# A 64-byte-aligned front operand, a normed operand 128 bytes further on, and two output projection tiles computed side by side

## The chip, the cores and the metric

The kernel runs on one core of a Trainium2 chip. The metric is the device time of one execution in microseconds (us); lower is better. The three runs of the kernel before gave 942.79, 944.01 and 944.62 us, so a median of 944.01 us.

## What is computed

One encoder block on 256 tokens of width 1024 in float32. Cut to what matters here:

```
n      = RMSNorm(x) * norm_mix
proj   = n @ w_in                                # 1024 x 5120: qA kA vA qB kB vB gA gB
yA, yB = differential attention, neighbourhood attention
merged = sigmoid(gA) * (yA @ w_proj_a) + sigmoid(gB) * (yB @ w_proj_b)
h      = x + merged @ w_out                      # the output projection
n2     = RMSNorm(h) * norm_ffn
q      = n2 @ peer_w_query                       # product-key router, top 16 of 16384 experts, 8 heads
y      = sum over the chosen experts of g * gelu(n2 . u_e) * v_e     # u, v: 16384 x 1024
out    = RMSNorm(h + y) * norm_final
```

The expert part is computed densely for 240 of the 256 tokens: all 128 tiles of 128 experts are multiplied with the normed tokens (the U stage), then all 128 tiles of `peer_v` with the gated results (the V stage). The other 16 tokens gather the rows of their own experts.

## The kernel before, in words

**Tiles.** All weights come as one stream of tiles, 8 chunks of 128 x 128 each, numbered `t`: tiles 0 to 39 input projection, 40 to 47 (`T_PROJ`) the two attention projections, 48 to 55 (`T_OUT`) the output projection, 56 to 71 (`T_QUERY`) the router's query, 72 to 199 (`T_U`) the U stage, then 128 tiles of the V stage. SyncE loads tile `t` into `raw` (4 slots). ScalarE makes its high part `whis` (L679), VectorE (L958) or GpSimd (L619) the remainder `wlos` = raw - high; both are rings of 4 slots. The moving operand of a stage is split in the same way, and TensorE computes three products a chunk: high x high, high weight x low operand, low weight x high operand. Each is one MATMUL with its own weight load (LDWEIGHTS), 24 of them a tile.

**Where these stand.** `split_product` (L1507) is the plain form: per chunk (whi, hi), (whi, lo), (wlo, hi), with 256 columns, or 240 in the first 42 and the last 2 tiles of the U stage. `halves_product` (L1515, L1516) is the wide form of U tiles 42 to 125: one MATMUL of 480 columns that takes high and low operand together against `whi` by the view `xpair[:, :, c, 0:NU]`, and one of 240 with `wlo`. L1819 and L1820 are the same two for the V stage, with the operand `vpair`. `token_tiles` (also L1507) turns the roles: for the V projections `xpair` is the weight and `whis`, `wlos` the moving operand.

**The operand `xpair`.** One buffer of 2 x 8 x 256 floats in each partition, high half then low half. In the front (tiles 0 to 39) it holds x scaled by the norm's gain, from tile 56 on it is written again with the normed tokens (`normed_hi` on ScalarE, `normed_low` on VectorE, through `xhi` and `xlo`), which the whole U stage reads. By the order of allocation its two halves start 192 bytes past a multiple of 256. `whis` and `wlos` start 128 past one, the operands of the projections and the query (`yhi`, `ylo`, `mhi`, `mlo`) 64 past one, `vpair` 128 past one. A chunk of 256 floats is 1024 bytes, so all chunks of an operand stand alike.

**The output projection.** Its moving operand is the merged, gated result, `mhi` and `mlo`, which VectorE and ScalarE make from each projection tile: after tile `k` VectorE runs two gating operations, the sum `mfull`, and after ScalarE's `mhi` (L786) the remainder `mlo` (L1152). The first tile, 48, is computed by `tile_arriving` (L1542, L1543, L1547): chunk by chunk, each product of `mhi` as it comes, the product of `mlo` two chunks later. Tiles 49 to 55 are plain. Tiles alternate between two PSUM banks, `pO[0]` and `pO[1]` (both halves of `pOO`), and each starts when its weights are ready (`lo_ready`) and VectorE has taken the last result of its bank (`evac_dve`, counted in `tile_wait`). After each tile VectorE adds the result to the residual in `xcol` (L1169), makes a `wlos` ahead (L958) and the low part of the next operand (L969); ScalarE makes the high part `yhi` (L691).

**PSUM.** Eight banks, in the pairs `pOO`, `pSS`, `pTT`, `pMM`. `pTT` (`pT[0]`, `pT[1]`) takes transposes in the attention and is free between the last of these and the router.

Of the kernel before, what the change touches and what calls it, by code (L numbers as in the profile page):

```python
# [27 lines left out]
F32 = mybir.dt.float32  # L28
F32R = mybir.dt.float32r
U32 = mybir.dt.uint32  # L30
ALU = mybir.AluOpType
ACT = mybir.ActivationFunctionType
AX_X = mybir.AxisListType.X

P = 128
T = 256
TB = T // P
D = 1024
C = D // P
# [5 lines left out]
PH, NK, TOPK = 8, 128, 16  # L45
# [13 lines left out]
T_OUT = T_PROJ + C  # L59
T_QUERY = T_OUT + C  # L60
# [5 lines left out]
RING = 4  # L66
# [7 lines left out]
UNITS_A, UNITS_B = 8, 8  # L74
# [33 lines left out]
NU = T - APART  # L108
# [5 lines left out]
OFFSETS_AT = 52  # L114
U_BUFS, V_BUFS = 4, 4
V_SLOT = 512
NG = NU - P
G_BLOCK = P + NK // RAW * NG
DOT_TILES = (3, 7, 16, 20, 28, 32, 41, 45)
# [61 lines left out]
def last_use(t):  # L181

    return max((x for x in range(t) if bank_of(x) == bank_of(t)), default=None)


def evac_engine(t):

    dve = lambda x: T_QB <= x < T_VB or T_GATE <= x < T_QUERY
    same = [x for x in range(t + 1) if dve(x) == dve(t)]
    return dve(t), len(same)  # L190
# [7 lines left out]
def build(nc, stream, urows, vrows, const, keys, bias, lamv, gfin, h1_dram, x_dram, a_dram, g_dram, out):  # L198
    with ExitStack() as top:
# [6 lines left out]
        def sbs(stack, name, shape, dt=F32):  # L206
            return stack.enter_context(nc.sbuf_tensor(name, shape, dt))
# [5 lines left out]
        whi = [whis[:, s] for s in range(RING)]  # L213
        wlo = [wlos[:, s] for s in range(RING)]

        with ExitStack() as front:
# [3 lines left out]
            xT = xcol[:, N_COL:N_COL + C * T].rearrange("p (c t) -> p c t", t=T)  # L220
# [8 lines left out]
            with ExitStack() as mixer:  # L229
                qkT = sbs(mixer, "qkT", [P, 16, T])  # L230
                gates = sbs(mixer, "gates", [P, 16, T])
# [36 lines left out]
                route = sbs(router, "route", [P, TB, 3, PH, TOPK])  # L268
                gsum = sbs(router, "gsum", [P, 2, TB, PH])
        G = sbs(top, "G", [P, RAW, G_BLOCK])  # L270
        held = sbs(top, "held", [P, 113, NK])
        vpair = sbs(top, "vpair", [P, RING, V_SLOT], F32R)
        small = sbs(top, "small", [P, T - P - 122, NK])
        hot_more = sbs(top, "hot_more", [P, GSUB, P], F32R)
# [27 lines left out]
        goff = small[:, 0, :].bitcast(U32)  # L302
        gval = small[:, 1, :].rearrange("p (h k) -> p h k", h=PH)
        fin = sbs(top, "fin", [P, 12])
        iota = sbs(top, "iota", [P, P])[:]
        with ExitStack() as uphase:
            xpair = sbs(uphase, "xpair", [P, 2, C, T], F32R)
            xhi, xlo = xpair[:, 0], xpair[:, 1]
            routeT = sbs(uphase, "routeT", [P, 3, P])
            ghiT = sbs(uphase, "ghiT", [P, P], F32R)  # L310
            hot1 = sbs(uphase, "hot1", [P, HOTS - 1, GSUB, P], F32R)
            ghot = sbs(uphase, "ghot", [P, HOTS - 1, GSUB, 2, P], F32R)
            ast = [sbs(uphase, f"ast{s}", [P, NU]) for s in range(AST)]
        with ExitStack() as vphase:
# [4 lines left out]
            epsc = sbs(vphase, "epsc", [P, 1])  # L319
            gfc = sbs(vphase, "gfc", [P, C])  # L320

        result = hT[:].rearrange("p (b x) t -> p b (x t)", b=TB)
        xtok = qpad[0:APART, 4:8, :].rearrange("p a t -> p (a t)")
        hots = [hot1[:, u] for u in range(HOTS - 1)] + [hot_more[:]]
# [62 lines left out]
        norm_hi = sem("norm_hi")  # L387
# [285 lines left out]
        def _(act):  # L673
# [22 lines left out]

            def normed_hi(c):
                act.wait_ge(normed, c + 1)
                act.activation(xhi[:, c, :], gates[:, c, :], ACT.Copy).then_inc(norm_hi, 1)

            def tanh_gate(j):

# [241 lines left out]
        def _(dve):  # L944
# [39 lines left out]
            def normed_low(c):  # L984
                dve.wait_ge(normed, c + 1)
                dve.wait_ge(norm_hi, c + 1)
                dve.tensor_tensor(xlo[:, c, :], gates[:, c, :], xhi[:, c, :].bitcast(F32), ALU.subtract).then_inc(norm_lo, 1)

            for half in range(2):
                dve.wait_ge(raw_landed[0] if half else head_landed, 16)  # L990
# [174 lines left out]
            for k in range(T_OUT, T_QUERY):  # L1165

                j = k - T_OUT
                dve.wait_ge(tile_done, k + 1)
                dve.scalar_tensor_tensor(xT[:, j, :], pO[k % 2][:, 0:T], 0.5, xT[:, j, :], ALU.mult, ALU.add).then_inc(evac_dve, 1)  # L1169
                dve.wait_ge(evac_dve, evac_engine(k)[1])  # L1170
                low_front(k + LEAD)
                gained_low(C, j)
                if j >= 2:
                    add_square(j - 1)
# [326 lines left out]
        def _(pe):  # L1501
            def split_product(dst, terms, opening=True, closing=True):

                last = None
                for c, (sh, sl, mh, ml) in enumerate(terms):
                    for q, (st, mv) in enumerate(((sh, mh), (sh, ml), (sl, mh))):
                        last = pe.matmul(dst, st, mv, start=(opening and c == 0 and q == 0), stop=(closing and c == len(terms) - 1 and q == 2))  # L1507
                return last
# [10 lines left out]
            def tile_wait(t):  # L1519

                pe.wait_ge(lo_ready, t + 1)
                if last_use(t) is not None:
                    by_dve, count = evac_engine(last_use(t))
                    pe.wait_ge(evac_dve if by_dve else evac_act, count)

            def tile(s, bank, mh, ml):

                return split_product(pO[bank][:, 0:T], [(whi[s][:, c, :], wlo[s][:, c, :], mh[:, c, :], ml[:, c, :]) for c in range(C)])

            def tile_arriving(t, mh, ml, high, low):  # L1530

                if last_use(t) is not None:
                    by_dve, count = evac_engine(last_use(t))
                    pe.wait_ge(evac_dve if by_dve else evac_act, count)
                s, dst = t % RING, pO[bank_of(t)][:, 0:T]
                last = None
                for c in range(C + WHOLE_LAG):
                    if c == 0:
                        pe.wait_ge(lo_ready, t + 1)
                    if c < C:  # L1540
                        pe.wait_ge(high[0], high[1] + c + 1)
                        pe.matmul(dst, whi[s][:, c, :], mh[:, c, :], start=c == 0, stop=False)  # L1542
                        pe.matmul(dst, wlo[s][:, c, :], mh[:, c, :], start=False, stop=False)  # L1543
                    e = c - WHOLE_LAG
                    if e >= 0:
                        pe.wait_ge(low[0], low[1] + e + 1)
                        last = pe.matmul(dst, whi[s][:, e, :], ml[:, e, :], start=False, stop=e == C - 1)  # L1547
                return last

            def token_tiles(s, bank, b):  # L1550
# [2 lines left out]
                return split_product(pO[bank][:, b * 2 * P:(b + 1) * 2 * P],  # L1553
                                     [(xhi[:, c, tok], xlo[:, c, tok], whis[:, s:s + 2, c, :], wlos[:, s:s + 2, c, :]) for c in range(C)])

            def square_sum(bank, k):

                pe.wait_ge(squares_added, k)
                ins = pe.matmul(bank[:, 0:T], ones[:], gates[:, 0, :], start=True, stop=k == 1)
                if k == 2:  # L1560
                    pe.wait_ge(squares, C + 1)
                    ins = pe.matmul(bank[:, 0:T], ones[:], gates[:, C - 1, :], start=False, stop=True)
                ins.then_inc(ssq_done, 1)
# [152 lines left out]
            for k in range(T_PROJ, T_OUT):  # L1716
# [3 lines left out]
                    last = split_product(pO[k % 2][:, half * T:(half + 1) * T],  # L1720
                                         [(whi[s][:, c, :], wlo[s][:, c, :], yhi[:, c, :], ylo[:, c, :]) for c in range(half * HA, (half + 1) * HA)])
                last.then_inc(tile_done, 1)
            for k in range(T_OUT, T_QUERY):
                if k == T_OUT:
                    tile_arriving(k, mhi, mlo, (m_hi, 0), (m_lo, 0)).then_inc(tile_done, 1)
                else:
                    tile_wait(k)
                    tile(k % RING, k % 2, mhi, mlo).then_inc(tile_done, 1)
            def score_keys(hp):
                if hp == 0:  # L1730
                    pe.wait_ge(keys_landed, 16)
# [48 lines left out]
            for i in range(NE_TILES):  # L1780
                if i == TURN_AT:
                    pe.wait_ge(routed, 1)
                    turn_route(1)
                k = g_step_at(i)
                s = (T_U + i) % RING
                wide_now = wide_tile(i)
                if i < WIDE_FIRST + 2:
                    tile_wait(T_U + i)
                else:
                    pe.wait_ge(lo_ready, T_U + i + 1)  # L1790
                    if i < WIDE_FIRST + 4:
                        pe.wait_ge(gbanks_free, 1)
                    else:
                        pe.wait_ge(halves_added, i - 4 - WIDE_FIRST + 1)
                dst = wide_u[(i - WIDE_FIRST) % 4] if wide_now else pO[i % 2]
                for half in range(1 if k is None else 2):
                    part = range(C) if k is None else range(half * C // 2, (half + 1) * C // 2)
                    if wide_now:
                        last = halves_product(dst, [(whi[s][:, c, :], wlo[s][:, c, :], xpair[:, :, c, 0:NU]) for c in part], 0 in part, C - 1 in part)
                    else:  # L1800
                        last = split_product(dst[:, 0:NU], [(whi[s][:, c, :], wlo[s][:, c, :], xhi[:, c, 0:NU], xlo[:, c, 0:NU]) for c in part], 0 in part, C - 1 in part)
                    if C - 1 in part:
                        last.then_inc(tile_done, 1)
                    else:

                        pe.wait_ge(gbanks_free, k + 1 if k >= 2 else 2)
                    if k is not None:
                        g_tokens(k, half)
                if i < 2:
                    score_keys(HP - 2 + i)  # L1810
# [165 lines left out]
```

## Time and profile before

| | |
|---|---|
| median of 3 runs | 944.01 us (942.79 to 944.62) |
| profiled execution, its own time | 944.44 us |
| its span, first to last instruction | 942.6 us |
| TensorE (PE) busy | 934.7 us, 99% of the span, 6660 MATMULs |
| TensorE weight loads (PEld) busy | 881.9 us, 94% |
| VectorE (DVE) busy | 783.7 us, 83% |
| ScalarE (ACT) busy | 580.4 us, 62% |
| GpSimd (POOL) busy | 343.6 us, 36% |
| mean granted clock of TensorE | 0.999 of full speed |
| chain of work that ended last | PE 94%, DVE 3%, issue 1%, ACT 1%, DMA 1% |

A MATMUL's time in the profile holds its way through the array and overlaps the next ones, so the busy time can't tell how fast products follow each other. What does is the distance from the start of one MATMUL to the start of the next, here called the **step**. It is read from start times in the timeline: over a long stretch, the difference of two starts divided by the number of MATMULs between them.

### The profile page before, as it was taken

Reading aid. Unit: us, or ns where it says so; the run is one execution under the profiler, and the core shown is the slowest. Engines: PE = TensorE matmul, PEld = TensorE weight load, DVE = VectorE, ACT = ScalarE, POOL = GpSimd, SP = SyncE. Lnnn points to the kernel's source line nnn. Section 1 sums busy time; section 2 is a strip of 40 time slices with the busy share of each in tenths; the row PEclk is TensorE's granted clock in tenths of the full one; section 3 lists DMA queues with packets and bytes.
Section 4 is the critical chain, followed back from the end, with each engine's and each line's share of the span. In section 5 each row is a group of like instructions: output and inputs, shape, how many; then the busy total and the mean of one; then the engine's idle time right before and its main releaser. Section 6 shows DMA issues by size and latency. Waiting matters only on the chain.

```text
span 942.6 us, 20282 instructions
## 1 busy us (share of the span) xinstructions
PE 934.7 (99%) x6660; PEld 881.9 (94%) x6660; DVE 783.7 (83%) x1578; ACT 580.4 (62%) x1078; POOL 343.6 (36%) x202
## 2 busy tenths in 40 slices
PE   9999999999999999999999999999999999999997
PEld 9999899999999999999999999999999999999997
DVE  7988877888799988888888987877788888888766
ACT  6555764656655547888788876655555555555545
POOL 0000000056878686888888877101100000010000
PEclk9999999999999999999999999999999999999999
DMA  8877668665688898999999998999999999999881
GB/s 300 267 235 217 202 199 237 199 218 194 186 252 234 242 255 193 254 284 285 229 257 291 236 258 248 320 346 319 319 313 319 344 330 319 319 326 313 290 267 46
DMA packets 133432, 246.55 MB, mean 262 GB/s; under 512 B 31136, under 2 KB 80160, under 8 KB 133104
## 3 DMA queue, kind: packets, MB, share of 16 engines
q1 hardware_dynamic: 110656, 227.73, 74.9%
q0 software_dynamic: 22272, 17.12, 9.5%
q8 instruction: 40, 0.66, 0.3%
q10 hardware_dynamic: 432, 0.80, 0.3%
q14 instruction: 32, 0.26, 0.1%
HBM read 219.21 MB, written 26.35 MB: 260 GB/s over the span
## 4 chain that ended last, share of the span: by engine, by line
PE 94%; DVE 3%; issue 1%; ACT 1%; DMA 1%; DVEq 0%; ACTq 0%
PE pOO L1507 29%; PE pMM L1515 8%; PE pOO L1515 8%; PE pTT L1819 6%; PE pMM L1819 6%; PE pOO L1819 6%; PE pSS L1819 6%; PE pOO L1516 4%; PE pMM L1516 4%; PE pOO L1820 3%; PE pMM L1820 3%; PE pTT L1820 3%; PE pSS L1820 3%; DVE wlos L958 1%; PE pSS L1581 1%
## 5 line engine op out<-in xcount | busy, mean ns | idle before, releaser
L679 ACT ACTIVATE whis<-raw 128x1024 fp32r<-128x1024 f32 x326 | 343.8, 1057 | 171.5 <-PE pSS L1820 145.1
L654 POOL DMA_INDIRECT g_scratch<-small x120 | 219.4, 1828 | 49.7 <-issue 35.1
L958 DVE TENSOR_TENSOR wlos<-raw,whis 128x1024 fp32r<-128x1024 f32 x172 | 208.9, 1218 | 20.0 <-ACT whis L679 19.1
L1386 DVE TENSOR_TENSOR wlos<-raw,whis 128x1024 fp32r<-128x1024 f32 x125 | 153.0, 1224 | 66.9 <-ACT whis L679 66.9
L1507 PE MATMUL pOO<-xpair,whis 128*128 128x240 f32 (+1 forms) x1184 | 205.6, 278 | 0.0
L1507 PEld LDWEIGHTS pOO<-xpair,whis 128*128 128x128 f32 x1184 | 179.0, 189 | 1.4 <-issue 1.4
L1507 PE MATMUL pOO<-xpair,wlos 128*128 128x240 f32 (+1 forms) x592 | 163.4, 276 | 0.0
L619 POOL TENSOR_TENSOR wlos<-raw,whis 128x1024 fp32r<-128x1024 f32 x30 | 72.2, 2414 | 214.4 <-ACT whis L679 214.3
L1515 PE MATMUL pMM<-xpair,whis 128*128 128x480 f32 x336 | 112.4, 379 | 0.0
L1507 PEld LDWEIGHTS pOO<-xpair,wlos 128*128 128x128 f32 x592 | 111.6, 188 | 0.0
L1515 PE MATMUL pOO<-xpair,whis 128*128 128x480 f32 x336 | 111.4, 379 | 0.0
L1516 PE MATMUL pOO<-xpair,wlos 128*128 128x240 f32 x336 | 91.2, 271 | 0.0
L1516 PE MATMUL pMM<-xpair,wlos 128*128 128x240 f32 x336 | 91.1, 271 | 0.0
L1819 PE MATMUL pTT<-vpair,whis 128*128 128x480 f32 x256 | 89.8, 375 | 0.0
L1819 PE MATMUL pMM<-vpair,whis 128*128 128x480 f32 x256 | 89.6, 374 | 0.0
L1819 PE MATMUL pOO<-vpair,whis 128*128 128x480 f32 x256 | 89.6, 374 | 0.0
L1819 PE MATMUL pSS<-vpair,whis 128*128 128x480 f32 x253 | 88.6, 374 | 0.0
L635 POOL DMA_INDIRECT held<-in_vrows,small x16 | 16.2, 1015 | 161.8 <-PE pSS L1820 161.8
L1515 PEld LDWEIGHTS pOO<-xpair,whis 128*128 128x128 f32 x336 | 63.1, 188 | 8.7
L1515 PEld LDWEIGHTS pMM<-xpair,whis 128*128 128x128 f32 x336 | 63.1, 188 | 8.3
L1820 PE MATMUL pOO<-vpair,wlos 128*128 128x240 f32 x256 | 70.4, 275 | 0.0
L1820 PE MATMUL pMM<-vpair,wlos 128*128 128x240 f32 x256 | 70.4, 275 | 0.0
(300 smaller groups left out, 2066.0 us busy)
## 6 DMA issues: line engine op xcount, KB each, us to landing
raw<-in_stream SPq DMA_DIRECT2D x199, 512.0 KB, 4.6
raw<-in_vrows SPq DMA_DIRECT2D x128, 512.0 KB, 4.7
a_scratch<-ast SPq DMA_DIRECT2D x128, 120.0 KB
held<-a_scratch SPq DMA_DIRECT2D x128, 120.0 KB, 4.8
g_scratch<-ghot SPq DMA_DIRECT2D x32, 256.0 KB, 4.3
G<-g_scratch SPq DMA_DIRECT2D x124, 64.0 KB, 4.5
biasm<-in_bias SPq DMA_DIRECT2D x8, 256.0 KB, 5.7
g_scratch<-small POOLq DMA_INDIRECT x128
```

Of the source, the lines that this page charges most:

```text
L619: pool.tensor_tensor(wlo[s], raw[s][:], whi[s].bitcast(F32), ALU.subtract).then_inc(lo_ready, 1)
L635: pool.indirect_dma_start(urow[U_BUFS + m % V_BUFS], None, picked, bass.IndirectOffsetOnAxis(uoff[:, m:m + 1], 0)).then_inc(urow_landed[U_ ...
L654: pool.indirect_dma_start(g_dram, bass.IndirectOffsetOnAxis(goff[:, n:n + 1], 0), gval[:, h, k:k + 1], None, compute_op=ALU.add).then_inc( ...
L679: act.activation(whi[s], raw[s][:], ACT.Copy).then_inc(hi_ready, 1)
L958: dve.tensor_tensor(wlo[t % RING], raw[t % RING][:], whi[t % RING].bitcast(F32), ALU.subtract).then_inc(lo_ready, 1)
L1386: dve.tensor_tensor(wlo[s], raw[s][:], whi[s].bitcast(F32), ALU.subtract).then_inc(lo_ready, 1)
L1507: last = pe.matmul(dst, st, mv, start=(opening and c == 0 and q == 0), stop=(closing and c == len(terms) - 1 and q == 2))
L1515: pe.matmul(both, sh, mv, start=opening and c == 0, stop=False)
L1516: last = pe.matmul(bank[:, 0:NU], sl, mv[:, 0, :], start=False, stop=closing and c == len(terms) - 1)
L1581: last = pe.matmul(pS[m][:, unit_columns(n)], qkT[rows, q0 + h, b * P:(b + 1) * P], qkT[rows, k0 + h, :], start=True, stop=True)
L1819: pe.matmul(wide[c], whi[s][:, c, :], gpair[s], start=opening, stop=False)
L1820: return pe.matmul(acc[c][:, 0:NU], wlo[s][:, c, :], ghi[s], start=False, stop=closing)
```

## The change

It has two parts.

**Where the operand starts.** The buffer becomes `xspan`, two rows of 8 x 256 + 32 floats, and a pad of 96 floats is put ahead of it. The front operand (`xhi`, `xlo`) begins each row, the normed operand (`xpair`) begins 32 floats (128 bytes) into each row. A row is now 8320 bytes instead of 8192. Counted past a multiple of 256 bytes:

| | front, high | front, low | normed, high | normed, low |
|---|---|---|---|---|
| before | 192 | 192 | 192 | 192 |
| now | 64 | 192 | 192 | 64 |

To make room `held` loses 4 rows that nothing reads, `iota` moves behind the operand, and `vpair`, `small` and the `hot_more` buffers move down by 2048 bytes, `hT` of the end by 2176 bytes; `hot1` and `ghot`, the operands of the 112 small products that build the gates (L1770), go from 192 to 64 past a multiple of 256. No instruction of the front or of the U and V stages is added, removed or moved.

**The output projection.** `mixed_tiles` computes tiles 48 and 49 chunk by chunk side by side, tile 48 into `pO[0]` and tile 49 into `pT[0]`. Tile 50 is plain again and goes to `pO[0]`.

```
+X_SHIFT, X_PAD = 32, 96
-        held = sbs(top, "held", [P, 113, NK])
+        held = sbs(top, "held", [P, 109, NK])
-        iota = sbs(top, "iota", [P, P])[:]
+        sbs(top, "x_pad", [P, X_PAD])
         with ExitStack() as uphase:
-            xpair = sbs(uphase, "xpair", [P, 2, C, T], F32R)
-            xhi, xlo = xpair[:, 0], xpair[:, 1]
+            xspan = sbs(uphase, "xspan", [P, 2, C * T + X_SHIFT], F32R)
+            iota = sbs(uphase, "iota", [P, P])[:]
...
+        xhi, xlo = [xspan[:, q, 0:C * T].rearrange("p (c t) -> p c t", t=T) for q in range(2)]
+        xpair = xspan[:, :, X_SHIFT:].rearrange("p q (c t) -> p q c t", t=T)
...
-                act.activation(xhi[:, c, :], gates[:, c, :], ACT.Copy).then_inc(norm_hi, 1)
+                act.activation(xpair[:, 0, c, :], gates[:, c, :], ACT.Copy).then_inc(norm_hi, 1)
...
-                dve.tensor_tensor(xlo[:, c, :], gates[:, c, :], xhi[:, c, :].bitcast(F32), ALU.subtract).then_inc(norm_lo, 1)
+                dve.tensor_tensor(xpair[:, 1, c, :], gates[:, c, :], xpair[:, 0, c, :].bitcast(F32), ALU.subtract).then_inc(norm_lo, 1)
...
-                dve.scalar_tensor_tensor(xT[:, j, :], pO[k % 2][:, 0:T], 0.5, xT[:, j, :], ALU.mult, ALU.add).then_inc(evac_dve, 1)
+                dve.scalar_tensor_tensor(xT[:, j, :], (pT[0] if j == 1 else pO[k % 2])[:, 0:T], 0.5, xT[:, j, :], ALU.mult, ALU.add).then_inc(evac_dve, 1)
...
+            def mixed_tiles():
+
+                two = (T_OUT, T_OUT + 1)
+                dst = [pO[0][:, 0:T], pT[0][:, 0:T]]
+                pe.wait_ge(evac_dve, evac_engine(last_use(T_OUT))[1])
+                pe.wait_ge(turned_taken, UNITS_A + UNITS_B)
+                for c in range(C - 1):
+                    for n, t in enumerate(two):
+                        if c == 0:
+                            pe.wait_ge(lo_ready, t + 1)
+                        pe.wait_ge(m_lo, c + 1)
+                        for q, (st, mv) in enumerate(((whi, mhi), (whi, mlo), (wlo, mhi))):
+                            pe.matmul(dst[n], st[t % RING][:, c, :], mv[:, c, :], start=c == 0 and q == 0, stop=False)
+                c = C - 1
+                pe.wait_ge(m_hi, C)
+                for n, t in enumerate(two):
+                    pe.matmul(dst[n], whi[t % RING][:, c, :], mhi[:, c, :], start=False, stop=False)
+                    pe.matmul(dst[n], wlo[t % RING][:, c, :], mhi[:, c, :], start=False, stop=False)
+                pe.wait_ge(m_lo, C)
+                for n, t in enumerate(two):
+                    pe.matmul(dst[n], whi[t % RING][:, c, :], mlo[:, c, :], start=False, stop=True).then_inc(tile_done, 1)
...
-            for k in range(T_OUT, T_QUERY):
-                if k == T_OUT:
-                    tile_arriving(k, mhi, mlo, (m_hi, 0), (m_lo, 0)).then_inc(tile_done, 1)
-                else:
-                    tile_wait(k)
-                    tile(k % RING, k % 2, mhi, mlo).then_inc(tile_done, 1)
+            mixed_tiles()
+            for k in range(T_OUT + 2, T_QUERY):
+                tile_wait(k)
+                tile(k % RING, k % 2, mhi, mlo).then_inc(tile_done, 1)
...
-                        last = split_product(dst[:, 0:NU], [(whi[s][:, c, :], wlo[s][:, c, :], xhi[:, c, 0:NU], xlo[:, c, 0:NU]) for c in part], 0 in part, C - 1 in part)
+                        last = split_product(dst[:, 0:NU], [(whi[s][:, c, :], wlo[s][:, c, :], xpair[:, 0, c, 0:NU], xpair[:, 1, c, 0:NU]) for c in part], 0 in part, C - 1 in part)
```

In the order of instructions the first place is TensorE where tile 48 ends and tile 49 begins. Before (`mhi`, `mlo` the operand, `whis`, `wlos` the weights; `m_hi`, `m_lo`, `lo_ready`, `evac_dve` the semaphores waited for):

```order
L1542 MATMUL pOO<-mhi,whis 128x256 [waits m_hi]
L1543 MATMUL pOO<-mhi,wlos 128x256
L1547 MATMUL pOO<-mlo,whis 128x256 [waits m_lo] x3
L1507 MATMUL pOO<-mhi,whis 128x256 [waits evac_dve,lo_ready]
L1507 MATMUL pOO<-mlo,whis 128x256
```

Here tile 48 waits for the last chunk of `mhi` and of `mlo` at its end, and tile 49 follows; the bank that tile 49 waits for was left by tile 47. The last two of `L1542` and its partner `L1543` are chunk 7.

The second place is TensorE at the end of the two tiles of the change and the start of tile 50 (`pOO` is tile 48, `pTT` tile 49):

```order
L1575 MATMUL pOO<-mhi,whis 128x256 [waits m_hi]
L1576 MATMUL pOO<-mhi,wlos 128x256
L1575 MATMUL pTT<-mhi,whis 128x256
L1576 MATMUL pTT<-mhi,wlos 128x256
L1579 MATMUL pOO<-mlo,whis 128x256 [waits m_lo]
L1579 MATMUL pTT<-mlo,whis 128x256
L1510 MATMUL pOO<-mhi,whis 128x256 [waits evac_dve,lo_ready]
L1510 MATMUL pOO<-mlo,whis 128x256
```

Chunk 7 now stands 42 MATMULs behind the start of tile 48 instead of 19, and between the last MATMUL of tile 48 (the first `L1579`) and tile 50, which needs that bank emptied, stands one other MATMUL. Before, a whole tile of 24 stood between two tiles of one bank.

## Rows read from the trace of the kernel before

**Rows 1.** The page: busy time, granted clock in 40 slices, chain that ended last.

```profile
PE 934.7 (99%) x6660; PEld 881.9 (94%) x6660; DVE 783.7 (83%) x1578; ACT 580.4 (62%) x1078; POOL 343.6 (36%) x202
...
PEclk9999999999999999999999999999999999999999
...
PE 94%; DVE 3%; issue 1%; ACT 1%; DMA 1%; DVEq 0%; ACTq 0%
```

**Rows 2.** Groups by form: line, engine, operation, shapes, count, busy us, mean ns, idle.

```profile
L1507 PE MATMUL pOO<-xpair,whis 128*128 128x240 f32 x704 | 118.6, 274 | 0.0
L1515 PE MATMUL pMM<-xpair,whis 128*128 128x480 f32 x336 | 112.4, 379 | 0.0
L1515 PE MATMUL pOO<-xpair,whis 128*128 128x480 f32 x336 | 111.4, 379 | 0.0
L1507 PE MATMUL pOO<-xpair,wlos 128*128 128x240 f32 x352 | 96.4, 274 | 0.0
...
L1507 PE MATMUL pOO<-xpair,whis 128*128 128x256 f32 x480 | 87.0, 282 | 0.0
```

**Rows 3.** Timeline of TensorE, input projection: start us, duration us, engine, line, operation.

```profile
12.71 0.39 PE L1507 MATMUL pOO<-xpair,whis 128*128 128x256 f32 x2
...
18.04 0.28 PE L1507 MATMUL pOO<-xpair,wlos 128*128 128x256 f32 x1
...
139.00 0.40 PE L1507 MATMUL pOO<-xpair,whis 128*128 128x256 f32 x2
```

**Rows 4.** Timeline of TensorE, tiles 40 to 56.

```profile
147.48 0.28 PE L1507 MATMUL pOO<-yhi,whis 128*128 128x256 f32 x1
...
170.09 0.28 PE L1542 MATMUL pOO<-mhi,whis 128*128 128x256 f32 x1
...
172.33 0.32 PE L1542 MATMUL pOO<-mhi,whis 128*128 128x256 f32 x1
...
173.02 0.28 PE L1507 MATMUL pOO<-mhi,whis 128*128 128x256 f32 x1
...
175.75 0.28 PE L1507 MATMUL pOO<-mhi,whis 128*128 128x256 f32 x1
...
178.36 0.28 PE L1507 MATMUL pOO<-mhi,wlos 128*128 128x256 f32 x1
...
192.07 0.28 PE L1542 MATMUL pOO<-yhi,whis 128*128 128x256 f32 x1
```

**Rows 5.** Timeline of TensorE, U stage, plain tiles: two tile starts, 29 tiles apart.

```profile
262.50 0.39 PE L1507 MATMUL pOO<-xpair,whis 128*128 128x240 f32 x2
...
340.23 0.39 PE L1507 MATMUL pOO<-xpair,whis 128*128 128x240 f32 x2
```

**Rows 6.** Timeline of TensorE, U stage, wide tiles.

```profile
520.25 0.38 PE L1515 MATMUL pOO<-xpair,whis 128*128 128x480 f32 x1
520.47 0.27 PE L1516 MATMUL pOO<-xpair,wlos 128*128 128x240 f32 x1
...
521.56 0.38 PE L1515 MATMUL pMM<-xpair,whis 128*128 128x480 f32 x1
```

**Rows 7.** Timeline of TensorE, V stage.

```profile
700.03 0.37 PE L1819 MATMUL pTT<-vpair,whis 128*128 128x480 f32 x1
700.25 0.28 PE L1820 MATMUL pTT<-vpair,wlos 128*128 128x240 f32 x1
...
701.34 0.37 PE L1819 MATMUL pOO<-vpair,whis 128*128 128x480 f32 x1
```

**Rows 8.** Timeline of VectorE around tiles 47 and 50.

```profile
172.31 0.43 DVE L1152 TENSOR_TENSOR mlo<-mfull,mhi 128x256 fp32r<-128x256 f32 x1 [0.55 <-ACT mhi L786]
...
178.67 0.42 DVE L1169 SCALAR_TENSOR_TENSOR xcol<-pOO,xcol 128x256 f32<-128x256 f32 x1 [0.63 <-PE pOO L1507]
```

**Rows 9.** Timeline of ScalarE: the last `mhi`, and `yhi` after tile 50.

```profile
171.79 0.42 ACT L786 ACTIVATE mhi<-mfull 128x256 fp32r<-128x256 f32 x1 [1.47 <-DVE mfull L1147]
...
179.13 0.51 ACT L691 ACTIVATE yhi<-xcol 128x256 fp32r<-128x256 f32 x1 [0.95 <-DVE xcol L1169]
```

## The prediction

> **What bounds the kernel now.** The page first [rows 1]: TensorE is busy 99% of the span at full granted clock in every slice, and it is 94% of the chain that ended last. VectorE, the next, is at 83% and 3% of the chain. So what counts is how fast TensorE's MATMULs follow each other, and how often they stand still. The groups by form [rows 2] say how many read the operand that is moved. In the U stage these are 704 + 352 = 1056 plain products of 240 columns (44 tiles) and 2 x 336 = 672 pairs of a 480-column and a 240-column product (84 tiles). In the input projection there are 40 tiles of 24, that is 960 products, 480 of them in the one group shown.
>
> Then the timeline, for the step from one start to the next.
>
> - Input projection, tiles 2 and 3: 12.71 to 18.04 us is 47 steps, 5.33 / 47 = 113.4 ns [rows 3]. Tiles 37 to 39: from 139.00 to 147.48 us are 72 steps, 8.48 / 72 = 117.8 ns [rows 3, 4]. Both at 192 bytes past a multiple of 256.
> - Attention projections, operand at 64: 147.48 to 170.09 us, 192 steps of 117.8 ns. Output projection from tile 49 on, also at 64: 173.02 to 192.07 us, 168 steps of 113.4 ns [rows 4].
> - U stage, plain: 262.50 to 340.23 us, 29 tiles or 696 steps, 111.7 ns [rows 5]. Wide: 520.25 to 521.56 us, four pairs, 1.31 / 4 = 0.327 us a pair; within a pair 0.22 for the wide product and 0.11 for the narrow one [rows 6].
> - V stage, operands at 128 and (narrow) 64: 700.03 to 701.34 us, four pairs, again 0.327 us a pair, again 0.22 and 0.11 [rows 7].
>
> So a 256-column product has two steps, 113.4 and 117.8 ns, and each of them occurs at 64 and at 192. It keeps one over many tiles and changes only where TensorE has stood still: tile 48 is the break between the long run at 117.8 and the long run at 113.4. And a pair takes 0.327 us at two quite different placings. That is the main fact for this change: these rows show a state that is entered at a stall, not a price of an address.
>
> **The output projection.** Before: tile 48 from 170.09 to 173.02 us is 2.93 us, and 24 steps of 117.8 ns would be 2.83, so 0.10 us was lost waiting for the last chunk of `mhi` and `mlo` (`mlo` is made from 172.31 to 172.74 us). Tile 49 ends at 175.75 us [rows 4, 8]. Now: chunk 7 is asked for 42 steps after 170.09 us, at 175.0 us, when its two parts have long been ready; that 0.10 us goes. The other added waits are for earlier events (the weights of tile 49 were made a tile earlier, the transposes are over) and cost nothing; were tile 49's weights late by some tenths, they would stall its first product by as much. The 48 products take 48 x 117.8 ns = 5.65 us, to 175.74 us.
>
> Then comes a new wait. Tile 50 goes into the bank of tile 48, whose last product started two steps before, at 175.51 us. VectorE takes a tile 0.31 us after its last start (178.36 to 178.67 us) [rows 4, 8]. From there to the engine released by it are 0.46 us (178.67 to 179.13 us) [rows 8, 9]. ScalarE's `mhi` ended at 172.21 us and the product waiting for it started at 172.33 us, 0.12 us later [rows 4, 9]; of the 0.46 us, 0.43 is the operation. So tile 50 starts at about 175.51 + 0.31 + 0.43 + 0.12 = 176.37 us, against 175.75 before: **+0.6 us**. TensorE stands for that time; nothing else hides it, as TensorE is the chain. Queued behind on VectorE are tile 49 and the `wlos` of tiles 51 and 52; it was idle 0.63 us before it took tile 50 [rows 8], so it has that much slack a tile, makes up the delay within two tiles, and I charge nothing. If it did not, tile 52 would wait for its weights by what is left, some tenths. If the 48 products went at 113.4 ns, tile 50 would start at 176.16, +0.4 us. If the tiles from 50 to 56, 168 products, fell back from 113.4 to 117.8 ns because the kick at 172.33 us is gone, that is 0.74 us more, +1.35 us in all. I take +0.6, since TensorE still gets a break there, a longer one than before.
>
> **The front operand.** 36 of its 40 tiles (all but 0 to 3) could be concerned, 864 products. Bounds: all of them go from 117.8 to 113.4 ns, 864 x 4.4 ns = -3.8 us. Or the ones that run at 113.4 now lose it: tiles 2 and 3 and the few like them, taken as five tiles, 120 x 4.4 = +0.5 us. I take 0, because the two placings, 64 and 192, stand in the rows with both steps.
>
> **The normed operand.** The high half stays at 192, only the low half goes to 64. The plain products: a step of 113.4 or 117.8 needs 256 columns, so bounds are 1056 x (117.8 - 111.7) = +6.4 us, and 1056 x (111.7 - 110) = -1.8 us, 110 being the 0.11 of the narrow product in the pairs. The pairs: the wide product could take the V stage's share without giving its narrow one's; the starts are read to 10 ns, so 672 x 5 ns = 3.4 us either way. I take 0 for both, because the sum of a pair came out alike for 192/192 and for 128/64. The V stage's 1024 pairs stay at 128 and 64, their buffer moves by a multiple of 256: 0. The 112 small products of the gates move from 192 to 64: at 4.4 ns each 0.5 us either way, taken as 0.
>
> **Sum.** 0 + 0 + 0.6 us. The profiled execution's own time of 944.44 us becomes 945.04; it stands 0.4 us over the median of the runs, so against that median it is 944.01 + 0.6 = **944.6 us**.
>
> **Rules weighed against it.** A 256-column product costs 117.8 or 113.4 ns here, and the difference is what the change could win. The Trainium skill, TensorE: Matmul & The Clock Gate, Back-to-back issue gap, gives N / 2.4 + 2.5 ns, for 256 columns 109.2 ns. The trace never reaches it in these stages; were the placing alone to blame for the rest, an estimate from that page would be 864 x 8.6 ns = 7.4 us in the front.
>
> The pairs cost the same at two placings and the 256-column products show both steps at either. The same skill, SBUF — State Buffer, Who interferes with whom, says that TensorE reads moving operand and weights through two independent ports and never waits on anyone. By that rule the placing cannot matter and the sum is the new wait alone; the trace agrees as far as 64 and 192 go, and leaves unexplained why there are two steps at all.
>
> **Rivals.**
>
> 1. *The placing does act, in the front or in the U stage* (faster). For it: something makes 4.4 ns between the two steps, the weights stand at 128, and operand and weight stream at once; high and low half at different placings is a case that no row shows. Against: the 117.8 of tiles 40 to 47 at 64. If most of the front goes to 113.4: -3.8 x 0.8 = -3.0, with the wait -2.4, so 941.6 us. If the pairs gain 5 ns instead: -3.4 + 0.6, 941.2 us. Both: 938.2 us.
> 2. *The low half at 64 slows the U stage* (slower, over 945.9 us). One mechanism: the plain product's step, now 111.7 ns, goes to the state of 117.8 because two of three products now read at different placings. Full price +6.4 + 0.6, 951.0 us; at half the tiles 947.8 us. It decides once the step exceeds 111.7 by 1.3 ns (1.3 us over 1056 products). Against: the narrow product of the V stage reads at 64 and its pair is no longer.
> 3. *The states fall otherwise*: nothing depends on the placing, but each break gets another outcome. Front -1 to +0.5 us, output projection +0.4 to +1.35 us: 943.5 to 945.9 us. This is within the forecast's side.
> 4. *The new wait isn't there*, if TensorE needed no fresh bank. The order speaks against it; the time would be 943.9 us, no measurable change either.
>
> **How the numbers follow.** 0.2% of this kernel, 1.9 us, is what a measurement can tell from no change. The forecast with rivals 3 and 4: 0.45. Rival 1: 0.35. Rival 2: 0.20. The predicted time is the forecast's, 944.6 us. Its own range is 943.5 to 945.9. The range for 8 in 10 takes in rival 1 to somewhat under its two single sizes, 940.8, which leaves out the double one (about 0.1), and rival 2 to nearly half its tiles, 947.5, which leaves out about 0.1.
>
> **What would show it.** Right: tile 50 starts 0.6 us later than 175.75 counted from tile 48's start, with TensorE waiting for VectorE's L1172 on `pOO`; the waits at the end of tile 48 are gone; the mean of the front's 256-column products with `whis` stays near the 282 ns of before [rows 2]; pairs still take 0.327 us, and 29 plain U tiles 77.7 us. Wrong: a front whose mean falls by some 4 ns with a step of 113.4 throughout; pairs under 0.322 or over 0.332 us; a plain U step other than 111.7.

## The result and the profile after

| | before | changed |
|---|---|---|
| median of 6 runs | 943.44 us (942.57 to 944.62) | 947.65 us (947.21 to 948.27) |
| profiled execution, own time | 944.44 us | 947.26 us |
| its span | 942.6 us | 945.4 us |

The ratio is 1.0045 with an interval of 1.0032 to 1.0058: the change costs 4.2 us, between 3.0 and 5.5. The forecast was 944.6 us and its range ended at 947.5.

The page after, the same lines as in [rows 1]:

```profile
PE 937.0 (99%) x6660; PEld 882.4 (93%) x6660; DVE 784.6 (83%) x1578; ACT 581.2 (61%) x1078; POOL 344.1 (36%) x202
...
PEclk9999999999999999999999999999999999999999
...
PE 94%; DVE 3%; issue 1%; ACT 1%; DMA 1%; DVEq 0%; ACTq 0%
```

Nothing there says what happened: the same engine bounds the kernel, at the same clock, over the same number of instructions. The groups by form, which answer to [rows 2], say a little more. Lines have moved by three (L1515 is now L1518, L1507 L1510), `xpair` is now called `xspan`:

```profile
L1518 PE MATMUL pOO<-xspan,whis 128*128 128x480 f32 x336 | 113.1, 382 | 0.0
...
L1510 PE MATMUL pOO<-xspan,whis 128*128 128x256 f32 x480 | 87.4, 284 | 0.0
```

The 480-column products into `pOO` last 382 ns on the mean instead of 379. A mean duration moves by less than the step does, so the step has to be read from starts. The timeline of TensorE in wide tiles after the change, where [rows 6] had four pairs in 1.31 us:

```profile
543.54 0.38 PE L1518 MATMUL pOO<-xspan,whis 128*128 128x480 f32 x1
...
544.87 0.38 PE L1518 MATMUL pOO<-xspan,whis 128*128 128x480 f32 x1
```

Four pairs take 1.33 us. The whole wide stage, from its first product to the first one of the V stage, before:

```profile
359.80 0.38 PE L1515 MATMUL pOO<-xpair,whis 128*128 128x480 f32 x1
...
597.77 0.38 PE L1819 MATMUL pTT<-vpair,whis 128*128 128x480 f32 x1
```

and after:

```profile
359.50 0.38 PE L1518 MATMUL pOO<-xspan,whis 128*128 128x480 f32 x1
...
600.55 0.38 PE L1842 MATMUL pTT<-vpair,whis 128*128 128x480 f32 x1
```

237.97 us have become 241.05, that is +3.1 us. Two such rows a stage give the whole account, and every stage time below is read in this way. Times are in us, from the first MATMUL of a stage to the first of the next. The front counts from the start of the span, "two" is the start of tile 48 to the start of tile 50, the query holds the router too, the wide stage also holds the last two plain tiles, and "V and end" goes to the start of the last MATMUL:

| run | front | attn. proj. | two | tiles 50-55 | query | U plain | U wide | V and end |
|---|---|---|---|---|---|---|---|---|
| before | 147.48 | 22.61 | 5.66 | 16.32 | 53.38 | 114.35 | 237.97 | 339.63 |
| changed | 147.47 | 22.61 | 6.31 | 16.41 | 52.18 | 114.52 | 241.05 | 339.64 |
| difference | -0.01 | 0.00 | +0.65 | +0.09 | -1.20 | +0.18 | +3.08 | +0.01 |

The differences add up to +2.8 us, as the two spans do. The medians say 4.2, so this pair of profiles flatters the change. The column to distrust is the query, where nothing was changed and 1.2 us went away.

The output projection looks as forecast. TensorE, then VectorE:

```profile
175.50 0.28 PE L1579 MATMUL pOO<-mlo,whis 128*128 128x256 f32 x1
176.39 0.36 PE L1510 MATMUL pOO<-mhi,whis 128*128 128x256 f32 x1 [0.49 <-DVE xcol L1172]
```

```profile
175.82 0.42 DVE L1172 SCALAR_TENSOR_TENSOR xcol<-pOO,xcol 128x256 f32<-128x256 f32 x1 [1.82 <-PE pOO L1579]
```

The two tiles run through, VectorE takes tile 48 as soon as it is there, and tile 50 waits for it until 176.39 us. Before it started at 175.75 us [rows 4].

Two accounts of the +3.1 us stand against each other. **Placing**: the pair of a 480- and a 240-column product costs more because the normed operand's low half stands elsewhere against the weights. **State**: TensorE is in a slower state there, handed on from the new stall, and the placing has nothing to do with it.

### The profile page after: what moved, and what is told of

Same layout as the page of the kernel before. It is cut to its first block, busy times and chain, and to the rows that moved or that the text cites. A ratio compares the mean times of both kernels' runs of the same rounds, so it can differ in the third digit from the quotient of the medians.

```text
span 945.4 us, 20283 instructions
## 1 busy us (share of the span) xinstructions
PE 937.0 (99%) x6660; PEld 882.4 (93%) x6660; DVE 784.6 (83%) x1578; ACT 581.2 (61%) x1078; POOL 344.1 (36%) x202
## 4 chain that ended last, share of the span: by engine, by line
PE 94%; DVE 3%; issue 1%; ACT 1%; DMA 1%; DVEq 0%; ACTq 0%
PE pOO L1510 29%; PE pOO L1518 8%; PE pMM L1518 8%; PE pTT L1842 6%; PE pMM L1842 6%; PE pOO L1842 6%; PE pSS L1842 6%; PE pOO L1519 4%; PE pMM L1519 4%; PE pOO L1843 3%; PE pMM L1843 3%; PE pTT L1843 3%; PE pSS L1843 3%; DVE wlos L961 1%; PE pSS L1606 1%
## 5 line engine op out<-in xcount | busy, mean ns | idle before, releaser
L1510 PE MATMUL pOO<-xspan,whis 128*128 128x240 f32 (+1 forms) x1184 | 206.2, 279 | 0.0
L1510 PEld LDWEIGHTS pOO<-xspan,whis 128*128 128x128 f32 x1184 | 179.4, 189 | 1.4 <-issue 1.4
L1510 PE MATMUL pOO<-xspan,wlos 128*128 128x240 f32 (+1 forms) x592 | 164.1, 277 | 0.0
L1518 PE MATMUL pMM<-xspan,whis 128*128 128x480 f32 x336 | 113.7, 381 | 0.0
L1518 PE MATMUL pOO<-xspan,whis 128*128 128x480 f32 x336 | 113.1, 382 | 0.0
L1510 PEld LDWEIGHTS pOO<-xspan,wlos 128*128 128x128 f32 x592 | 112.4, 190 | 0.0
L1519 PE MATMUL pOO<-xspan,wlos 128*128 128x240 f32 x336 | 92.2, 274 | 0.0
L1519 PE MATMUL pMM<-xspan,wlos 128*128 128x240 f32 x336 | 92.0, 274 | 0.0
L1518 PEld LDWEIGHTS pOO<-xspan,whis 128*128 128x128 f32 x336 | 64.1, 191 | 9.5
L1518 PEld LDWEIGHTS pMM<-xspan,whis 128*128 128x128 f32 x336 | 63.8, 190 | 8.9
L1843 PE MATMUL pTT<-vpair,wlos 128*128 128x240 f32 x256 | 70.4, 275 | 0.0
```

Source lines behind the costliest of these rows:

```text
L1518: pe.matmul(both, sh, mv, start=opening and c == 0, stop=False)
L1519: last = pe.matmul(bank[:, 0:NU], sl, mv[:, 0, :], start=False, stop=closing and c == len(terms) - 1)
L1843: return pe.matmul(acc[c][:, 0:NU], wlo[s][:, c, :], ghi[s], start=False, stop=closing)
```

## The experiments

**One part each.** The placing alone takes the output projection back to that of before:

```
-            mixed_tiles()
-            for k in range(T_OUT + 2, T_QUERY):
-                tile_wait(k)
-                tile(k % RING, k % 2, mhi, mlo).then_inc(tile_done, 1)
+            for k in range(T_OUT, T_QUERY):
+                if k == T_OUT:
+                    tile_arriving(k, mhi, mlo, (m_hi, 0), (m_lo, 0)).then_inc(tile_done, 1)
+                else:
...
```

Expected:

> The change's placing alone (front 64/192, normed 192/64 past a multiple of 256, for high/low half); the output projection as before. Theory 'placing': the wide pairs of the U stage take 0.332 to 0.333 us instead of 0.327, 672 of them make +3.2 us, the output projection takes as long as before, so about 946.6 us against 943.4. Rival 'state': the slower pair is a state that the new stall at tile 50 handed on; then pairs are back at 0.327 us here and the time is that of before within 1 us.

Measured: 947.93 us against 943.85, ratio 1.0041 (1.0029 to 1.0053), 1.3 us more than the 946.6 expected. The wide stage took 241.31 us, and every stage ahead of the U stage took what it did before, within 0.04 us:

```profile
359.96 0.38 PE L1518 MATMUL pOO<-xspan,whis 128*128 128x480 f32 x1
...
601.27 0.38 PE L1844 MATMUL pTT<-vpair,whis 128*128 128x480 f32 x1
```

The other part alone is the kernel before with `mixed_tiles` put in. Expected:

> Tiles 48 and 49 side by side alone, every buffer where it was. Theory 'placing': pairs stay at 0.327 us; tile 50 starts 0.7 us later than before, and the query tiles get back up to 1.1 us as in the changed kernel (they read the same operand at the same place), so 943.0 to 944.2 us. Rival 'state': pairs take 0.332 us and the time is near 946.6 us.

Measured: 944.52 us against 943.85, ratio 1.0011 (1.0002 to 1.0019), so about +1 us and 0.3 us above the expected range. The wide stage took 237.98 us. The wait at tile 50 is there as in the changed kernel:

```profile
175.13 0.28 PE L1576 MATMUL pTT<-mlo,whis 128*128 128x256 f32 x1
175.90 0.36 PE L1507 MATMUL pOO<-mhi,whis 128*128 128x256 f32 x1 [0.49 <-DVE xcol L1169]
```

So the wide stage's +3.1 to +3.3 us belongs to the placing and comes without the new stall; the state theory falls. The two parts' ratios, +0.41% and +0.11%, add up to the whole's +0.45% within their intervals.

**Which half, and against what.** Next the row length: with 64 floats behind each row instead of 32, high and low half stand alike, front 64/64 and normed 192/192.

```
-            xspan = sbs(uphase, "xspan", [P, 2, C * T + X_SHIFT], F32R)
+            xspan = sbs(uphase, "xspan", [P, 2, C * T + X_ROW], F32R)      # X_ROW = 64
```

> As the first, but each row is 256 bytes longer than 8 x 256 floats, so high and low half stand alike: front 64/64, normed 192/192. Theory 'placing of the low half': pairs are back at 0.327 us, the plain U tiles at 2.680 us, and the time at that of before, 943.4 us (a front at 64/64 changes it by less than 1 us). Rival 'the row length or the move of the buffer as such costs': pairs stay at 0.332 us, 946.6 us.

Measured: 943.92 us, ratio 0.9995 (0.9986 to 1.0004); the wide stage took 238.35 us:

```profile
359.12 0.37 PE L1518 MATMUL pOO<-xspan,whis 128*128 128x480 f32 x1
...
597.47 0.38 PE L1844 MATMUL pTT<-vpair,whis 128*128 128x480 f32 x1
```

The buffer has moved, the rows are longer, the front stands at 64, and the loss is gone. `hot1` and `ghot`, the operands of the small products that build the gates, stand at 64 here as in the changed kernel, so they are not the cause either. What is left is the place of the normed low half.

Without shift and without the longer row all four stand at 64:

> Rows of 8 x 256 floats, everything at 64: front 64/64, normed 64/64. Theory 'it is the difference between high and low half': pairs at 0.327 us, time of before. Rival 'it is 64 as such': pairs at 0.333 us or more, 947 us or more.

Measured: 946.96 us, ratio 1.0033 (1.0021 to 1.0044), wide stage 240.67 us. Halves that stand alike are not enough.

> Front and normed operand both at 64 (high half) and 192 (low half), output projection as before. Theory 'the low half's place sets the pair' (it is the second block of the 480-column product): pairs back at 0.327 us, time of before, 943.9 us. Rival 'any half at 64 costs': pairs at 0.331 to 0.333 us, 946.5 to 947.5 us.

Measured: 946.90 us, ratio 1.0044 (1.0028 to 1.0061), wide stage 240.09 us. The rival holds: a half at 64 costs, the high one too.

> Every half at 128, where the weights whis and wlos stand as well, rows of 8 x 256 floats. Theory 'it is the distance between operand and weights': at distance 0 the starts of both streams fall together; if that collides, pairs of 0.333 us or more and 947 us or more. Rival 'only 64 is bad': 0.327 us and 943.9 us. The V stage's wide product starts at 128 and its pairs take 0.327 us, which speaks for the rival.

Measured: 945.92 us, ratio 1.0029 (1.0017 to 1.0042), wide stage 238.23 us. Pairs are back at 0.327 us, so for them equal places of operand and weights cost nothing. What the run lost lies in other stages: front +1.8 us, tiles 48 to 55 +1.4 us, V stage and end +0.6, attention projections -0.8. The front's share can be read from its last three tiles, 72 steps, where the kernel before took 8.48 us or 117.8 ns a step [rows 3, 4]:

```profile
140.62 0.40 PE L1510 MATMUL pOO<-xspan,whis 128*128 128x256 f32 x2
...
149.26 0.29 PE L1510 MATMUL pOO<-yhi,whis 128*128 128x256 f32 x1
```

Here they take 8.64 us, 120.0 ns a step. That is neither of the two steps of before: the place costs the 256-column products too, and distance 0, which is good for the pairs, is bad for them.

> Every half at a multiple of 256. Theory 'distance': 128 from the weights, as far as can be; pairs at or under 0.327 us, at best 0.320, 939 to 944 us. Rival 'each placing is its own case': no figure beyond 0.320 to 0.335 us a pair.

Measured: 948.36 us, ratio 1.0058 (1.0041 to 1.0075), wide stage 240.35 us. The theory that far apart is good falls, and the time is 4 us above its range.

Then everything from the weights on was moved by 128 bytes, so that no distance between these buffers changed modulo 256:

```
+        sbs(top, "w_pad", [P, 32])
         whis = sbs(top, "whis", [P, RING, C, P], F32R)
...
-        held = sbs(top, "held", [P, 113, NK])
+        held = sbs(top, "held", [P, 112, NK])
```

> The kernel before with 128 bytes of pad ahead of the weight rings, so that weights, normed operand and everything behind them move together: weights at 0, normed 64/64, vpair at 0. Theory 'distance between operand and weights': the distance is that of before (64), so the wide pairs take 0.327 us, the U and V stage 352 and 340 us, the time is that of before, 943 to 944 us. Rival 'absolute place': 64/64 costs 0.331 us a pair as it did with the weights at 128, 2.7 us more, 946 us.

Measured: 943.53 us, ratio 1.0003 (0.9993 to 1.0012). The normed operand stands at 64/64, which cost 2.7 us in the run with everything at 64, and the wide stage took

```profile
358.01 0.38 PE L1516 MATMUL pOO<-xpair,whis 128*128 128x480 f32 x1
...
596.24 0.38 PE L1820 MATMUL pTT<-vpair,whis 128*128 128x480 f32 x1
```

238.23 us. Two single distances between pairs, 464 and 438 ns at 407.63 us, account for 0.25 us of this. There a weight load waits for VectorE's `wlos`:

```profile
408.10 0.19 PEld L1516 LDWEIGHTS pMM<-xpair,whis 128*128 128x128 f32 x1 [0.27 <-DVE wlos L959]
```

The run with longer rows has two such places (401 to 525 ns, 0.48 us together; one at the same wait, the other with no releaser in the profile). The placing alone has one, at the same wait, 0.26 us. These are no price of the pair's placing.

The same absolute place is slow with the weights at 128 and fast with the weights at 0. **What counts is where the moving operand stands relative to the weights.** Strictly, the run shows this for the weights together with all buffers behind them, which moved along. That it is the weights among these is argued from the pairs reading nothing else.

Three more mixes, and one finer step:

> Front 64/128, normed high half at 192, low half at 0. Theory 'the pair is slow when a half stands at 64 or 0 (64 or 128 behind the weights)': 0.330 us or more, 946 us. Rival 'both halves have to stand alike': 0.331 us too; this run and the next tell these two apart.

> Front 64/0, normed high half at 192, low half at 128. Theory 'a half at 64 or 0 is slow, at 128 or 192 it isn't': pairs at 0.327 us or below, 942.5 to 944 us. Rival 'both halves have to stand alike': 0.331 us, 946.5 us.

> Front and normed operand at 128 (high) and 192 (low). Theory 'a half at 64 or 0 is slow': pairs at 0.327 us; the front and the query pay up to 1.8 us for the steps they fall into, as with all at 128, 943.5 to 946 us. Rival 'alike': pairs at 0.331 us, 946.5 us or more.

> Front and normed operand, both halves, 32 bytes past the weights' place (160 past a multiple of 256). The pairs took 0.327 us at distances 0 and 64. Theory 'lines of 64 bytes': 32 behaves as 0 does or worse by a split line, 0.327 to 0.331 us. Rival: a pair under 0.325 us, which would be a version to keep, 942 us or less.

Measured, in this order: 947.00 us, ratio 1.0039 (1.0025 to 1.0053); 946.96 us, 1.0039 (1.0027 to 1.0052); 948.92 us, 1.0060 (1.0044 to 1.0077); 947.81 us, 1.0051 (1.0034 to 1.0068). No run's pairs came under 0.325 us on the mean. The theory "0 or 64 for either half is fine" falls with the second and third of them, whose halves both stand at good places, but at different ones. All runs together, by distance (operand's place less the weights' place, modulo 256), with the mean distance of starts over the 672 pairs, from one wide product to the second product behind it:

| high / low, bytes from the weights | run | ns a pair | U wide, us | U plain, us |
|---|---|---|---|---|
| 64 / 64 | before | 327.0 | 237.97 | 114.35 |
| 64 / 64 | longer rows | 327.5 | 238.35 | 114.35 |
| 64 / 64 | all moved | 327.3 | 238.23 | 114.35 |
| 0 / 0 | all at 128 | 327.3 | 238.23 | 114.38 |
| 32 / 32 | all at 160 | 329.6 | 239.73 | 115.46 |
| 128 / 128 | all at 0 | 330.5 | 240.35 | 114.35 |
| 192 / 192 | all at 64 | 331.0 | 240.67 | 114.69 |
| 64 / 0 | 192 and 128 | 330.0 | 240.00 | 114.67 |
| 64 / 128 | 192 and 0 | 330.2 | 240.09 | 114.53 |
| 192 / 64 | 64 and 192 | 330.2 | 240.09 | 115.27 |
| 64 / 192 | the change | 331.8 | 241.05 | 114.52 |
| 0 / 64 | 128 and 192 | 331.9 | 241.33 | 115.24 |

Without the single long distances told above, the longer rows give 326.8 ns and the run with all moved 327.0. For the pairs two placings are fast, 0/0 and 64/64. Every mixed one, and 32, 128 and 192, cost 2.6 to 4.9 ns a pair. The place kept by the kernel before is the best of those tried.

The extra time isn't with one product of the pair. From the wide product's start to the narrow one's the change takes 219.1 ns instead of 217.2, from there to the next wide one 112.6 instead of 109.8, though the narrow product reads the high half, which did not move.

The front's last three tiles sort by distance too, but otherwise. Their step is 117.8 ns in every run whose front halves stand 64 or 192 from the weights. It is 116.7 at 32/32, 118.6 at 128/128, 118.8 at 192/128, 119.3 at 192/0, and 120.0 at 0/0 and 0/64. In the five runs from 118.6 on, the attention projections, whose own operand never moved, took 21.8 us instead of the 22.61 of all others. So the step there follows how the front ended. The gain was lost again: tile 48 then waited 0.6 us for ScalarE's `mhi`, and "two" took 6.35 to 6.47 us.

**The new wait.** The side-by-side part with tile 50 in the fourth free bank, so that it waits only for its weights:

```
+                if k == T_OUT + 2:
+                    pe.wait_ge(lo_ready, k + 1)
+                else:
+                    tile_wait(k)
+                out_tile(k, {T_OUT + 2: pT[1]}.get(k, pO[k % 2])).then_inc(tile_done, 1)
```

> Placing of before, tiles 48 and 49 side by side, and tile 50 into the free bank pT[1], so that it does not wait for the bank of tile 48. Theory 'the 0.6 us of the side-by-side part is that wait': tile 50 starts at 175.7 us counted as in the kernel before, 0.65 us earlier than with the side-by-side part alone; the rest depends on which step tiles 50 to 71 fall into, 942.5 to 944.5 us. Rival 'the two tiles themselves are slower': tile 50 starts late all the same.

Measured: 943.90 us against 943.11, ratio 1.0011 (1.0002 to 1.0021). The wait is gone:

```profile
175.81 0.28 PE L1581 MATMUL pTT<-mlo,whis 128*128 128x256 f32 x1
175.93 0.28 PE L1507 MATMUL pTT<-mhi,whis 128*128 128x256 f32 x1
```

"Two" takes 5.65 us again, 0.66 less than with the wait, as expected. But tiles 50 to 55 take 16.96 us instead of 16.32: they stayed at the step of 117.8 ns, where the kernel before had dropped to 113.4 after its short waits at the end of tile 48. Against the kernel before that is +0.64 us, as much as the wait had cost, and the ratio is the same as with the wait. That it follows from the missing break is not shown, and other runs speak against it as a rule. The side-by-side kernel has the break, and its first profile reads 17.03 us there, its second 16.42. Four of the placing runs (all at 128, all at 0, 64 and 192, 192 and 0) have the output projection of before, and took 16.96 us.

**What a profile draws.** The kernel before, unchanged, was profiled twice more, and the side-by-side part once more:

> The kernel before, unchanged, profiled once more. Theory 'the query's time is drawn anew in every execution': its stage differs from the 53.4 us of the first profile in at least one of this run and the next (52.0 to 53.4 us), the wide pairs keep 0.327 us. Rival 'it follows from the code': 53.4 us again.

> The kernel before, unchanged, a third profile: same expectations as the run ahead of it.

> The side-by-side part alone, profiled once more. The wait at tile 50 is in the code, so tiles 48 and 49 take 6.3 us to the start of tile 50 again. If the query's time is drawn anew, it may differ from 52.0 us; if it follows from the code, 52.0 us again.

| run | own time | front | two | tiles 50-55 | query | U plain | U wide | V and end |
|---|---|---|---|---|---|---|---|---|
| before, 1st | 944.44 | 147.48 | 5.66 | 16.32 | 53.38 | 114.35 | 237.97 | 339.63 |
| before, 2nd | 942.60 | 147.00 | 5.67 | 16.32 | 51.98 | 114.35 | 237.98 | 339.64 |
| before, 3rd | 943.31 | 147.53 | 5.67 | 16.32 | 52.16 | 114.35 | 237.98 | 339.64 |
| side by side, 1st | 943.98 | 146.98 | 6.31 | 17.03 | 51.98 | 114.35 | 237.98 | 339.67 |
| side by side, 2nd | 943.53 | 147.15 | 6.31 | 16.42 | 52.00 | 114.35 | 237.98 | 339.67 |

The query stage starts in the first profile at 192.07 us [rows 4]; its end, the first product of the U stage, and then both rows in the second profile of the same kernel:

```profile
245.45 0.47 PE L1507 MATMUL pOO<-xpair,whis 128*128 128x240 f32 x2
```

```profile
191.61 0.28 PE L1542 MATMUL pOO<-yhi,whis 128*128 128x256 f32 x1
...
243.59 0.47 PE L1507 MATMUL pOO<-xpair,whis 128*128 128x240 f32 x2
```

53.38 and 51.98 us. So the query is drawn anew: a stretch of 256-column products falls into one of the two steps from one execution to the next. The U and V stages repeat to 0.01 us for one and the same kernel in these profiles. A difference of 0.2 us there has a cause, though it can be a late weight tile as above, so the distances within the pairs have to be looked at. One of 1.4 us in the query means nothing. The first profile of before had drawn the slow query, which is why the two profiles stood only 2.8 us apart. The stages that repeat give 0.65 + 0.18 + 3.08 = 3.9 us, in the interval of the measured 4.2.

## Why the prediction was wrong

**The normed operand's pairs: the step that failed.** The prediction put 672 x 5 ns = 3.4 us either way as the bound and took 0, "because the sum of a pair came out alike for 192/192 and for 128/64". Measured: 331.8 - 327.0 = 4.8 ns a pair, 672 x 4.8 = +3.2 us (the whole stage +3.1), nearly the bound. The size was in the text; the value taken was wrong. The V stage's pair was no evidence: its operand is one run of 480 floats that starts with the weights (distance 0) and has its second half 960 bytes on (distance 192), with no second row of its own place, and the U stage's are two runs. Equal results at two points were read as if the placing did not matter, when both were among the few good ones. The prediction had itself named high and low half at different placings as a case that no row showed, but used that for the faster rival alone; the slower rival was pinned on the plain products, whose share turned out +0.18 us. That rival's headline came true, its mechanism did not. The prediction's own alarm, pairs over 0.332 us, would have let these 331.8 ns pass: at 672 pairs a bound of 5 ns is too wide to notice 3 us.

**"A state that is entered at a stall, not a price of an address".** Right for the 256-column products at the places 64 and 192 that the rows had, and wrong for the pairs. Both exist: the two steps of 113.4 and 117.8 ns are drawn, and the price of the distance is fixed. For the 256-column products it was luck that the change moved the front between these two places; at 0 or 128 bytes from the weights its last tiles took 118.6 to 120.0 ns a step.

**The independent read ports.** The rule weighed there, that TensorE never waits on anyone (the Trainium skill, SBUF — State Buffer, Who interferes with whom), would have given no effect of the placing. These runs disagree: at equal code and work, moving the operand 128 bytes against the weights changes the pair from 327 to 331 ns, and moving both together does not. The measurement decides. By what way the distance acts is not shown, nor that the ports themselves are where it does.

**The output projection: right.** Forecast: tile 50 at 176.37 us, +0.6. Measured: 176.39 us, "two" +0.65, in all of the kernels with that part, and away with the bank exchanged. The waits at the end of tile 48 went as said. VectorE caught up by tile 52 and nothing more was late.

**The front: right in the sum.** -0.01 us in the pair of profiles. It reads 147.0 to 147.5 us in three profiles of before, and 146.8 twice with front 64/64; those 0.2 us aren't settled, as the first product of the front starts anywhere from 5.4 to 6.0 us in these runs. Nothing of the 3.8 us of the faster rival came.

**The chances.** Slower had 0.2 and the range ended 0.15 us under the measured median. The slower case was priced on one mechanism with its sum at 947.8 for half of it; had the pairs' bound of 3.4 us stood there beside the sure +0.6 (944.01 + 4.0 = 948.0 us), the range would have held the time. Some luck is in that: the base of 944.01 us, the median of three runs, stood 0.6 us over the 943.44 of six.

## What to carry to other kernels

Where products stream with a weight load each, look at the distance between the moving operand and the weights, and keep the halves of a wide product that stand in two rows at one and the same good distance. For the pairs here 0 and 64 bytes modulo 256 were good, all others tried cost 0.7% of the stage or more; for the 256-column products 0 was bad (+1.8 us in the front), so 64 alone was good for both. Before trusting a difference between two profiles, know which stages repeat: profile the same kernel twice, and read the change from those. Where a row shows equal costs at two placings, a third placing is still untested. And a tile that goes side by side with another needs its bank's successor free as well, or the wait only moves behind the pair.

## What the runs showed of the hardware

- The step of back-to-back MATMULs with a weight load each depends on the place of the moving operand relative to the weights (and the buffers that move with them) modulo 256 bytes: 327.0 to 331.9 ns a pair of 480 and 240 columns, the stage of one kernel repeating to 0.01 us in 238, and also between 0, 32 and 64 bytes (327.3, 329.6, 327.0).
- For 256-column products the distance has other prices: 116.7 ns at 32 bytes, 117.8 at 64 and 192, 118.6 at 128, 120.0 at 0, in the last three tiles of the front.
- 256-column products have two steps, 113.4 and 117.8 ns, at one and the same placing, and a stretch of them may keep either; it changed after TensorE had stood, as at tile 48 of the kernel before (117.8 to 113.4). The query stage of one unchanged kernel took 53.38, 51.98 and 52.16 us.
- The granted clock was 0.998 to 1.0 in all profiled executions, at the level of 2.4 GHz, and explains none of it.
